# Cross-attention keys in full fp32, made from unsplit weights in pieces between the mixer's small matmuls; the memory scaled once

## The chip, the cores and the metric

The kernel runs on one core of one Trainium2 chip. The metric is device time in microseconds of one execution; one span of the profile is one execution on that core. The program is written engine by engine (TensorE, VectorE, ScalarE, GpSimd, SyncE), with its own order of work on each and semaphores between them.

## The reference, cut to what matters

Two layers of a decoder trunk, for 256 prompt positions and 8 x 4 sample positions (288 columns together), model width 1024:

```
for l in range(DEPTH):                                   # DEPTH = 2
    x = x + 0.5 * swiglu_ffn(rmsnorm(x, ffn1_norm[l]), ...)
    h = rmsnorm(x, mix_norm[l])
    x = x + concat(conv | dilated attention | rwkv7)(h @ w_in[l]) @ w_out[l]
    h  = rmsnorm(x, xattn_norm[l])
    hm = rmsnorm(mem, mem_norm[l])                       # mem (256, 1024): the same in both layers
    mk, mv = split(hm @ w_kv[l], 2, axis=-1)             # keys and values, 1024 columns each; both also outputs
    x = x + cross_attend(h, mk, mv, w_q[l], w_o[l])      # 4 heads of 256, over the 256 memory rows
    x = x + 0.5 * swiglu_ffn(rmsnorm(x, ffn2_norm[l]), ...)
```

`rmsnorm(mem, g)` is `mem * (1 / sqrt(mean(mem**2) + eps)) * g`: only the gain `g` differs from layer to layer. The sample rows take their memory keys and values from caches.

## The kernel before, in words

Everything is held transposed: 128 channels on the partitions, positions along the free axis, so `x` is 8 tiles of 128 x 288 and the memory 8 tiles of 128 x 256. Weights stream in as slabs of 1 MB (128 x 2048 fp32), in one order written out in `ORDER`, through a ring of four slots: SyncE issues slab n when what stood in its slot, slab n-4, has been released, and waits for that before it goes on to the next (L490). A weight slab holds two units of 128 x 1024. ScalarE rounds a unit to a short fp32 form `w_hi` (`CAST w_hi<-slots`) and VectorE makes the rest, `w_lo`; there are three pairs of buffers for them, two more for some units of `out`. The activations are split likewise, and a product is three matmuls: hi by hi, lo by hi, hi by lo (`mm3`, L691 to L693). A split slab is released by VectorE's `w_lo` of its second unit; a slab that is read as it is (the caches `wink`, `winv`, `memk`, `memv`) by TensorE's last matmul on it. `columns` (L744) runs one output tile after another: 8 x `mm3` into a PSUM bank.

The order of one layer on TensorE: ffn1; the mixer's in-projection; the mixer itself, which is small matmuls (rwkv state updates L961 to L1110, convolution and group-norm statistics L1118 to L1150, attention scores L1168, transposes `turn_probs` L1178, `apply_probs` L1189, sample attention on the cached windows L1202 and L1271); then `out_part` and `columns("out")`; then cross attention: key tiles 0 to 3 (`memory_keys`, by `columns`), `sum_squares("xattn")` between the first two, query tiles 0 to 7, the other key tiles, the scores (L1343), the values with the sample scores among them (L1328), softmax, `sample_values` (L1397), the output projection, and ffn2. The small matmuls wait often for ScalarE and VectorE, which evict, exponentiate and normalise between them.

The memory is normalised where the mixer ends. Its squares are summed in the first layer only, by eight full fp32 matmuls between the attention steps (L1224, `memory_squares`). In both layers VectorE then multiplies by root and gain (`normalise("mem", ...)`, L1994 to L2002) and makes `hm_lo` while TensorE does the window values and the first out tiles; the wait for `attn_lo` (the last attention rows' low part), which the attention tiles of `out` need, comes after this in VectorE's order. Full fp32 matmuls appear as two instructions each on TensorE; `x` counts in the trace are of instructions.

Of the kernel before, what the change touches and what calls it, by code (L numbers as in the profile page):

```python
# [38 lines left out]
K_BANKS = (1, 2, 3, 6, 0, 7)  # L39
V_BANKS = (6, 7, 6, 7, 0, 1, 2, 3)  # L40
# [13 lines left out]
MEMK_EARLY = 6  # L54
K_EARLY = 4
# [14 lines left out]
CACHES = ("wink", "winv", "memk", "memv")  # L70
ORDER = [(_name, _i) for _name, _n in STAGES for _i in range(_n)]
# [4 lines left out]
for _i in range(K_EARLY // 2):  # L76
    ORDER.remove(("kv", _i))
    ORDER.insert(ORDER.index(("q", 0)), ("kv", _i))

for _i in range(MEMK_EARLY):  # L80
    ORDER.remove(("memk", _i))
    ORDER.insert(ORDER.index(("kv", _i + K_EARLY // 2)) + 1, ("memk", _i))
PARKED = tuple(("memv", _i) for _i in range(4))
PARKED_BEHIND = {("kv", 4): (0, 1, 2), ("kv", 7): (3,)}
# [6 lines left out]
for _n, (_name, _i) in enumerate(ORDER):  # L91
    if _name not in CACHES:
        UNITS.setdefault(_name, NUNIT)
        UNIT_OF_SLAB[_n] = NUNIT
        NUNIT += 2


def kv_unit(i):
    return UNIT_OF_SLAB[SLAB_AT["kv", i // 2]] + i % 2
# [6 lines left out]
EXTRA_AT = 16384  # L106
# [138 lines left out]
def program(nc, x_in, mem_in, stream, small, consts, conv_hist, wkv_in, copies, outs, known=None):  # L245
    (y_out, conv_out, kv_out, shift_out, wkv_p_out, wkv_s_out, memk_out, memv_out) = outs
    known = known or {}
    with ExitStack() as ctx:
# [26 lines left out]
        rs = sb("rs", [P, T])  # L275
        halves = sb("halves", [P, 2 * J])[:]
# [41 lines left out]

        top[0] = KT * T
        qx = take(KT, T)  # L320
        h_flat, sq_flat = h_mem.rearrange("p a k t -> p (a k t)"), sq.rearrange("p k t -> p (k t)")
        parked = (sq_flat[:, 0:SLAB], h_flat[:, 0:SLAB], h_flat[:, SLAB:2 * SLAB])
# [3 lines left out]

        memx = sq.rearrange("p k t -> p (k t)")[:, 0:KT * MEM].rearrange("p (k t) -> p k t", k=KT)
        top[0] += KT * T
        hm_lo = over("hm_lo", top[0], KT, MEM)
        hm = take(KT, MEM)  # L330
        oxs = hm.rearrange("p k t -> p (k t)")[:, 0:256]
        kx = take(KT, MEM)
        parked += (kx.rearrange("p k t -> p (k t)"),)
        xq_lo = over("xq_lo", top[0], KT, T)
        vx = take(2, 4 * MEM)
        pxT = take(4, 2, TP)
        px = take(9, MEM)


        w_more = tuple(over(name, EXTRA_AT + i * UNIT, UNIT)[:] for i, name in enumerate(("w_more_hi", "w_more_lo")))  # L340
        qz = take(KT, DEC_BATCH * 36)
        qz_own = qz.rearrange("p k (b c) -> p k b c", b=DEC_BATCH)[:, :, :, 0:DEC_SEQ]
        xstat = take(4, 9)
# [72 lines left out]
        assert top[0] <= after_solve  # L416
        top[0] = after_solve
# [36 lines left out]
        mem_landed = sem("mem_landed")  # L454
        parked_landed = [sem(f"parked_landed{i}") for i in range(len(PARKED))]
# [60 lines left out]
        def _(pool):  # L516
# [7 lines left out]
            def presum(l, tag, n):  # L524

                for k in range(1, n):
# [3 lines left out]
                    PL.done(nc.gpsimd.tensor_tensor(sq[:, 0, :], sq[:, 0, :], sq[:, k, :], ALU.add), (tag, "added", k))  # L530
# [3 lines left out]
            for l in range(DEPTH):  # L534
# [3 lines left out]
                if l == 0:  # L538
                    pool.wait_ge(con_landed, 48)

# [34 lines left out]
                pool.wait_ge(scalar_done, SL.value(l, ("u", 1)))  # L575
                pool.dma_start(memx, mem_in).then_inc(mem_landed, 16)
# [18 lines left out]
                pool.wait_ge(vector_done, VL.value(l, ("x_out", 0)))  # L595
                pool.wait_ge(stored, store_value(l, "wkv_s"))
                PL.done(nc.gpsimd.memset(qz, 0.0), "qz_clear")
                presum(l, "xattn", PRESUM["xattn"])
                pool.wait_ge(scalar_done, SL.value(l, ("kx", KT - 1)))
# [61 lines left out]
        def _(pe):  # L661
# [6 lines left out]
            for l in range(DEPTH):  # L668
# [37 lines left out]

                def ffn(tag):
                    for t in range(FT):
# [3 lines left out]
                        for b, o in ((gb, 0), (ub, 1)):  # L712
# [9 lines left out]
                            TL.done(i, (tag, "up" if o else "gate", t))  # L722
                            if (t, o) == ((1, 0) if tag == "ffn1" else (0, 0)):
                                sum_squares(tag)
# [238 lines left out]

                pe.wait_ge(vector_done, VL.value(l, "primed"))
# [41 lines left out]
                for j in range(J):  # L1006
                    for hh in range(2):
# [14 lines left out]
                TL.done(i, ("tok", 2, 2))  # L1022
                claim(5, (SL, ("o", 2)))
                pe.wait_ge(wkv_landed, 16 * l + 16)
                for j in range(J):
# [9 lines left out]
                    else:  # L1035
                        turn(2 + j)
                def value_rows(ct):
# [33 lines left out]
                TL.done(i, "s_xinc")  # L1071
                value_rows(1)
# [12 lines left out]
                claim(7, (SL, ("u", 2)))  # L1085
                pe.wait_ge(scalar_done, SL.value(l, ("r", 2)))
                pe.wait_ge(vector_done, VL.value(l, "s_x"))
                for j in range(J):
                    for hh in range(2):
                        s_ = slice(j * P + hh * HD, j * P + (hh + 1) * HD)  # L1090
                        i = mm(bank[7][0:TS, s_], sm[0:TS, hh, 2, j * TS:(j + 1) * TS], rm2[0:TS, s_], start=True, stop=True)
                TL.done(i, ("u", 2))
                value_rows(2)
                pe.wait_ge(scalar_done, SL.value(l, ("u", 2)))
# [6 lines left out]
                TL.done(i, "s_o")  # L1101

# [11 lines left out]
                def conv_variance():  # L1114
                    claim(7, (SL, "ln_std"))
                    pe.wait_ge(scalar_done, SL.value(l, "conv_sq"))
                    for ch in range(2):
                        i = mm(bank[7][J * 32:, 0:T], ones[:, 0:32], yc2[:, ch, :], start=ch == 0, stop=ch == 1)  # L1118
# [10 lines left out]
                def ln_variance():  # L1129

                    pe.wait_ge(scalar_done, SL.value(l, "ln_sq"))
                    for j in range(J):
                        i = mm(bank[7][j * 32:(j + 1) * 32, 0:T], heads[:, HD - 16:HD + 16], tmp_ln[:, j, :], start=True, stop=True)
# [20 lines left out]
                conv_mean(1)  # L1154
                ln_mean()
                next_states(0)
                conv_variance()
                ln_variance()
                def scores(u):
# [1550 lines left out]
```

## Time and profile before

| | us |
|---|---|
| three runs, median (lowest to highest) | 1635.23 (1634.82 to 1640.63) |
| the profiled execution, span | 1636.5 |
| TensorE busy in it | 1582.2 (97%) |
| VectorE, ScalarE, GpSimd busy | 1067.9, 735.3, 231.4 |
| layer 0: mixer's small matmuls, scores to window values | 377.7 to 441 |
| layer 1: the same | 1182.6 to 1245 |

Stretches of the trace are given as from:to in us from the start of the span. A window's row gives its length, the busy time of every engine with its instruction count, the granted clock of TensorE as a share of full speed (1.00 is 2.4 GHz, 0.50 is 1.2 GHz), the busy share of the DMA engines and what they moved in GB/s. A row of a timeline gives start and length in us, the engine, line and operation, what it writes and reads, how many instructions were grouped, and in brackets the idle time before it with what ended that. A row of waits gives the engine and its line, what it waited for, and the total, the number and the longest of these waits in us. PEld is TensorE's weight load, which runs ahead of the matmuls. A row that groups a line's instructions gives its busy time and mean ns, and behind the bar the idle time before them.

### The profile page before, as it was taken

How to read it: one execution, taken by the hardware profiler on the slowest of the kernel's cores; microseconds unless marked ns; L12 is line 12 of the kernel's file. 1: busy time of each engine (PE TensorE's matmuls, PEld its weight loads, DVE VectorE, ACT ScalarE, POOL GpSimd, SP SyncE). 2: the span in 40 equal slices, each digit the busy share in tenths (PEclk: the TensorE clock that was granted, in tenths of full speed). 3: DMA queues.
4: the chain of work that ended last, by engine and by line, in shares of the span. 5: the costliest groups of instructions: out<-in, count | busy, mean ns of one | idle time of the engine just before them, and what ended most of it. 6: DMA issues, size and time to landing. Idle time of an engine off the chain costs nothing.

```text
span 1636.5 us, 31838 instructions
## 1 busy us (share of the span) xinstructions
PE 1582.2 (97%) x13578; PEld 1499.3 (92%) x13578; DVE 1067.9 (65%) x1654; ACT 735.3 (45%) x1233; POOL 231.4 (14%) x214
## 2 busy tenths in 40 slices
PE   8999999899899999999999999998999999999997
PEld 8999998896799789999999999998858987999997
DVE  5777466978764367775477754678786643777744
ACT  5444357523553354443354433573335434544433
POOL 1000000893010010000010000029801000100000
PEclk9999999998999999999999999999969999999999
DMA  6766754402647754445355667442135478544450
GB/s 228 274 237 251 287 182 136 142 3 87 228 175 284 302 215 162 173 155 181 134 191 204 242 251 282 136 148 86 35 125 206 169 304 319 187 158 176 156 175 35
DMA packets 39980, 303.66 MB, mean 186 GB/s; under 512 B 4832, under 2 KB 4992, under 8 KB 7424
## 3 DMA queue, kind: packets, MB, share of 16 engines
q1 hardware_dynamic: 37504, 288.88, 48.6%
q0 software_dynamic: 2048, 11.17, 2.0%
q8 instruction: 108, 1.77, 0.4%
q10 hardware_dynamic: 288, 1.57, 0.3%
q14 instruction: 32, 0.26, 0.0%
HBM read 291.85 MB, written 36.83 MB: 201 GB/s over the span
## 4 chain that ended last, share of the span: by engine, by line
PE 84%; DVE 8%; ACT 5%; DMA 1%; issue 1%; DVEq 0%; ACTq 0%
PE bank L691 23%; PE bank L693 22%; PE bank L692 22%; PE bank L877 3%; DVE w_lo L1982 2%; DMA slots<-stream 1%; ACT w_hi L1443 1%; PE bank L1397 1%; PE bank L1343 1%; PE bank L1328 1%; PE bank L1380 1%; PE bank L841 1%; PE bank L961 1%; PE bank L704 1%; PE bank L1202 1%
## 5 line engine op out<-in xcount | busy, mean ns | idle before, releaser
L1982 DVE TENSOR_TENSOR w_lo<-slots,w_hi 128x1024 fp32r<-128x1024 f32 x386 | 482.1, 1251 | 339.0 <-ACT w_hi L1443 338.7
L1443 ACT CAST w_hi<-slots 128x1024 fp32r<-128x1024 f32 x390 | 405.9, 1044 | 338.6 <-PE bank L693 298.5
L691 PE MATMUL bank<-h_hi,w_hi 128*128 128x288 f32 x1808 | 540.7, 299 | 13.9 <-DVE h_lo L1941 4.8
L692 PE MATMUL bank<-h_lo,w_hi 128*128 128x288 f32 x1808 | 535.2, 296 | 0.0
L693 PE MATMUL bank<-h_hi,w_lo 128*128 128x288 f32 x1808 | 533.4, 295 | 0.0
L691 PEld LDWEIGHTS bank<-h_hi,w_hi 128*128 128x128 f32 x1808 | 340.6, 188 | 20.4 <-DVE w_lo L1982 5.8
L693 PEld LDWEIGHTS bank<-h_hi,w_lo 128*128 128x128 f32 x1808 | 342.2, 189 | 0.0
L692 PEld LDWEIGHTS bank<-h_lo,w_hi 128*128 128x128 f32 x1808 | 341.3, 189 | 0.3
L693 PE MATMUL bank<-hid_hi,w_lo 128*128 128x288 f32 x704 | 207.7, 295 | 0.0
L692 PE MATMUL bank<-hid_lo,w_hi 128*128 128x288 f32 x704 | 207.3, 294 | 0.0
L691 PE MATMUL bank<-hid_hi,w_hi 128*128 128x288 f32 x704 | 207.1, 294 | 0.0
L1443 ACT COPY arena<-bank 128x256 f32<-128x256 f32 (+7 forms) x224 | 77.5, 378 | 216.7 <-PE bank L693 89.7
L530 POOL TENSOR_TENSOR arena<-arena 128x288 f32<-128x288 f32 x45 | 41.5, 922 | 875.9 <-ACT arena L1493 873.6
L693 PEld LDWEIGHTS bank<-hid_hi,w_lo 128*128 128x128 f32 x704 | 132.1, 188 | 0.0
L691 PEld LDWEIGHTS bank<-hid_hi,w_hi 128*128 128x128 f32 x704 | 132.0, 188 | 0.0
L692 PEld LDWEIGHTS bank<-hid_lo,w_hi 128*128 128x128 f32 x704 | 132.0, 188 | 0.0
L1512 ACT ACTIVATE arena<-arena 128x288 f32<-128x288 f32 x88 | 39.2, 445 | 188.0 <-DVE arena L2021 188.0
L557 POOL TENSOR_SCALAR arena<-arena,par_all 128x256 f32<-128x256 f32 x88 | 101.2, 1161 | 3.9
L2021 DVE TENSOR_TENSOR arena<-bank,rs 128x288 f32<-128x288 f32 x88 | 40.3, 458 | 38.9 <-PE bank L693 38.2
L877 PE MATMUL bank<-arena 64*64 64x64 f32 x1488 | 55.6, 228 | 8.6 <-DVE arena L2251 7.3
L877 PEld LDWEIGHTS bank<-arena 64*64 64x64 f32 x1488 | 52.8, 142 | 11.2 <-DVE arena L2251 7.7
L573 POOL TENSOR_TENSOR arena<-arena 128x512 f32<-128x512 f32 x44 | 61.4, 1395 | 0.3
(350 smaller groups left out, 2274.0 us busy)
## 6 DMA issues: line engine op xcount, KB each, us to landing
slots<-stream SPq DMA_DIRECT2D x235, 1024.0 KB, 5.0
out_win3k<-win3k SPq DMA_DIRECT2D x2, 4080.0 KB
out_win3v<-win3v SPq DMA_DIRECT2D x2, 4080.0 KB
arena<-stream SPq DMA_DIRECT2D x4, 1024.0 KB, 8.1
h_mem<-stream SPq DMA_DIRECT2D x4, 1024.0 KB, 10.0
out_win2k<-win2k SPq DMA_DIRECT2D x2, 2032.0 KB
out_win2v<-win2v SPq DMA_DIRECT2D x2, 2032.0 KB
con<-consts SPq DMA_DIRECT2D x1, 2308.0 KB, 10.7
```

The costliest lines, as they stand in the source:

```text
L530: PL.done(nc.gpsimd.tensor_tensor(sq[:, 0, :], sq[:, 0, :], sq[:, k, :], ALU.add), (tag, "added", k))
L557: p_ = nc.gpsimd.tensor_scalar(out, up[:, ch, tap:tap + TP], w, None, ALU.mult)
L573: PL.done(nc.gpsimd.tensor_tensor(ycv[:, :, 0:TP], ycv[:, :, 0:TP], prod[:, tap % 2, :, 0:TP], ALU.add), ("summed", tap))
L691: mm(out, lhs[0], rhs[0], start=start, stop=False)
L692: mm(out, lhs[0], rhs[1], start=False, stop=False)
L693: return mm(out, lhs[1], rhs[0], start=False, stop=stop)
L704: i = mm(bank[7][:, 0:n], ones, squares[:, k, 0:n], start=k == 0, stop=k == KT - 1)
L877: i = mm(bank[b][o_, s_], lhs[r_, s_], rhs[r_, s_], start=True, stop=True)
L1443: return SL.done(nc.scalar.copy(out, in_), name)
L1512: SL.done(fn(th[:, t % 2, :], gs[:, t % 2, :], ACT.Tanh, scale=0.5), (tag, "tanh", t))
L1982: D(tt(out, src, hi.bitcast(F32), ALU.subtract), name)
L2021: D(tt(gs[:, t % 2, :], bank[gb][:, 0:T], rs[:], ALU.mult), (tag, "gated", t))
```

## The change

**Keys.** The first four `kv` slabs hold the keys' weights; they are now read whole, as the caches are. A key tile is eight matmuls in full fp32, with the 128 x 128 weights as they stand in the slot and the normalised memory `hm` (256 columns) moving. They are issued in pieces by `keys_on(n)` among the mixer's small matmuls, tile 7 first and tile 0 last: 24 before the first scores, 24 up to the last attention step, 8 in front of the wait for `attn_lo`, 8 after the out columns. All tiles but the last share bank 7; ScalarE's `keys_out(t)` copies a tile out, and the next one's first matmul waits for that. `columns("k", ...)`, its 24 matmuls per tile and the splits of its eight units go.

```
@@ TensorE
+                def keys_on(n):
+                    for _ in range(n):
+                        at, k = divmod(piece[0], KT)
+                        t = K_SEQ[at]
+                        b = 7 if at < KT - 1 else 1
+                        if k == 0:
+                            claim(b, (SL, ("kx", t)))
+                        if at == 0:
+                            pe.wait_ge(scalar_done, SL.value(l, ("mem", "h", k)))
+                        w = arrived(SLAB_AT["kv", t // 2]).rearrange("p (o k c) -> p o k c", o=2, k=KT)
+                        i = mm(bank[b][:, 0:MEM], w[:, t % 2, k, :], hm[:, k, :], start=k == 0, stop=k == KT - 1)
+                        piece[0] += 1
+                    if k == KT - 1:
+                        TL.done(i, ("k", "cols", t))
+                        if t % 2 == 0:
+                            TL.done(i, ("slab", SLAB_AT["kv", t // 2]))
...
+                keys_on(2)
                 claim(2, (SL, ("tok", 2, 0)))
...
                 TL.done(i, "s_o")
+                keys_on(2)
@@ ScalarE
+                def keys_out(t):
+                    act.wait_ge(tensor_done, TL.value(l, ("k", "cols", t)))
+                    copy(kx[:, t, :], bank[7 if t != K_SEQ[-1] else 1][:, 0:MEM], ("kx", t))
...
                 value_rows(2)
+                keys_out(6)
                 select(range(2, DEC_BATCH))
```

In TensorE's order this is the place in layer 0 around the sample rows' state (`s_o` is the group with 64x8x4), where a key tile ends and the next begins; before:

```order
L961 MATMUL bank<-arena,con 128x288
L1091 MATMUL bank<-arena 32x64 x6
L1041 MATMUL bank<-con,arena 32x128 x3
L1099 MATMUL bank<-arena 64x8x4 x6
L1049 MATMUL bank<-arena,con 128x288 x2
L1127 MATMUL bank<-arena,con 128x288 x3
```

The key pieces are L1018 in the changed kernel, with two of them behind `s_o`:

```order
L1002 MATMUL bank<-arena,con 128x288
L1018 MATMUL bank<-arena,slots 128x256 x3
L1157 MATMUL bank<-arena 32x64 x6
L1105 MATMUL bank<-con,arena 32x128 x3
L1018 MATMUL bank<-arena,slots 128x256 x2
L1166 MATMUL bank<-arena 64x8x4 x6
L1018 MATMUL bank<-arena,slots 128x256 x2
L1113 MATMUL bank<-arena,con 128x288 x2
L1018 MATMUL bank<-arena,slots 128x256 x2
L1195 MATMUL bank<-arena,con 128x288 x3
```

Eleven pieces have gone before; 3 and 2 complete the second tile (tile 6) ahead of `L1166`; the 17th and 18th behind it begin tile 5 in the same bank, and two more stand between two groups of statistics.

Further on in the same engine's order come the window scores (`slots,arena`), the first transposes and `apply_probs`; before:

```order
L1110 MATMUL bank<-arena 64x512 x2
L1202 MATMUL bank<-slots,arena 32x128 x28
L1178 MATMUL bank<-con,arena 128x128 x3
L1168 MATMUL bank<-arena 128x128 x3
L1189 MATMUL bank<-arena 64x128 x3
L1202 MATMUL bank<-slots,arena 32x128 x14
```

and in the changed kernel:

```order
L1178 MATMUL bank<-arena 64x512 x2
L1273 MATMUL bank<-slots,arena 32x128 x28
L1018 MATMUL bank<-arena,slots 128x256 x7
L1249 MATMUL bank<-con,arena 128x128 x3
L1239 MATMUL bank<-arena 128x128 x3
L1018 MATMUL bank<-arena,slots 128x256
L1260 MATMUL bank<-arena 64x128 x3
L1273 MATMUL bank<-slots,arena 32x128 x14
```

Seven pieces now stand in front of the transposes that wait for the first softmax, and one between the scores and the first `apply_probs`.

**Memory.** The sum of squares moves into ffn1 of layer 0: GpSimd loads the memory, ScalarE squares it, GpSimd adds, one matmul sums over the partitions behind gate tile 17, ScalarE takes the root, VectorE the reciprocal and the product, and GpSimd stores the scaled memory in DRAM once. In each layer ScalarE's queue loads it and ScalarE multiplies by the gain, among the rwkv evictions. The split of `hm`, which the values still use, moves to the out columns.

```
-                normalise("mem", memx, hm, mem_rs, MEM, (hm_hi, hm_lo), between_rows)
+                for u in range(2):
+                    split(UNITS["out"] + NW - 1 + u)
+                dve.wait_ge(scalar_done, SL.value(l, "attn_hi"))
+                low(h_lo[:, 2:2 + G, TP:T], h[:, 2:2 + G, TP:T], h_hi[:, 2:2 + G, TP:T], "attn_lo")
...
+                    dve.wait_ge(scalar_done, SL.value(l, ("mem", "h_hi", t)))
+                    low(hm_lo[:, t, :], hm[:, t, :], hm_hi[:, t, :], ("mem", "h_lo", t))
...
+                act.dma_start(hm, mem_scaled).then_inc(mem_landed, 16)
+                def memory_gained(tiles):
+                    for k in tiles:
+                        act.wait_ge(mem_landed, 16 * l + 16)
+                        g = PAR["mem"] + k
+                        SL.done(fn(hm[:, k, :], hm[:, k, :], ACT.Copy, scale=par_all[:, l, g:g + 1]), ("mem", "h", k))
```

**Order of slabs and values.** The key slabs go between the cache slabs; the values' first two slabs, kv4 and kv5, come before the queries, and the rest after them. Two value pairs are computed before the queries now; after the scores come sample scores 0 and 1, values 2, sample scores 2, values 3, sample scores 3 to 7 in a row.

```
-MEMK_EARLY = 6
-K_EARLY = 4
+MEMK_EARLY = 4
+K_SLABS, V_EARLY = 4, 2
...
+for _i, _next in ((3, ("wink", 0)), (2, ("wink", 2)), (1, ("winv", 0)), (0, ("out", 2))):
     ORDER.remove(("kv", _i))
+    ORDER.insert(ORDER.index(_next), ("kv", _i))
...
-PARKED_BEHIND = {("kv", 4): (0, 1, 2), ("kv", 7): (3,)}
+PARKED_BEHIND = {("kv", 6): (0, 1, 2), ("kv", 7): (3,)}
```

On SyncE the rows of layer 0 from the cache slabs to the parked `memv` slabs (`arena<-stream`, `h_mem<-stream`), with what each issue waits for, were:

```order
L490 DMA slots<-stream 128x2048 [waits vector_done] x20
L490 DMA slots<-stream 128x2048 [waits tensor_done] x8
L490 DMA slots<-stream 128x2048 [waits vector_done] x10
L501 DMA arena<-stream 128x2048 [waits tensor_done]
L501 DMA h_mem<-stream 128x2048 [waits tensor_done] x2
L490 DMA slots<-stream 128x2048 [waits tensor_done]
L490 DMA slots<-stream 128x2048 [waits vector_done]
```

and are now:

```order
L513 DMA slots<-stream 128x2048 [waits vector_done] x20
L513 DMA slots<-stream 128x2048 [waits tensor_done] x11
L513 DMA slots<-stream 128x2048 [waits vector_done]
L513 DMA slots<-stream 128x2048 [waits tensor_done]
L513 DMA slots<-stream 128x2048 [waits vector_done] x7
L524 DMA arena<-stream 128x2048 [waits tensor_done]
L524 DMA h_mem<-stream 128x2048 [waits tensor_done] x2
L513 DMA slots<-stream 128x2048 [waits vector_done]
L513 DMA slots<-stream 128x2048 [waits tensor_done]
L524 DMA arena<-stream 128x2048 [waits stored,tensor_done]
L513 DMA slots<-stream 128x2048 [waits tensor_done]
```

The single `tensor_done` row between two `vector_done` rows is kv5: it goes into the slot of kv0, which TensorE releases with the last key matmul; the four query slabs stand behind it in the queue. Behind kv7 now stand memk3 to memk7; before, memk5 to memk7.

**Banks.** `p_clear` moves from VectorE to GpSimd, the sample rows' `u` and the prompt rows of `apply_probs` use bank 6, the conv and norm variances bank 4, since bank 7 holds the keys.

## Rows read from the trace of the kernel before

**Rows 1.** The page: busy time of the engines, and the chain that ended last.

```profile
PE 1582.2 (97%) x13578; PEld 1499.3 (92%) x13578; DVE 1067.9 (65%) x1654; ACT 735.3 (45%) x1233; POOL 231.4 (14%) x214
...
PE 84%; DVE 8%; ACT 5%; DMA 1%; issue 1%; DVEq 0%; ACTq 0%
```

**Rows 2.** Windows: the mixer's small matmuls up to the first transposes, both layers.

```profile
377.70:414.40 36.70, 33.19 (x343) 21.59 (x342) 31.77 (x81) 16.00 (x33) 4.83 (x7) 0.81 0.40 127
...
1182.60:1222.00 39.40, 36.03 (x342) 23.38 (x342) 31.77 (x81) 16.00 (x33) 4.08 (x6) 0.74 0.36 119
```

**Rows 3.** Windows: the stretches of the mixer in which the clock stood at 0.50.

```profile
385.50:399.10 13.60, 13.60 (x72) 8.32 (x72) 11.20 (x35) 6.00 (x16) 2.38 (x5) 0.50 0.46 162
...
416.20:419.60 3.40, 3.40 (x31) 2.72 (x30) 3.33 (x7) 0.92 (x2) 0.24 (x1) 0.50 0.68 277
1187.60:1208.10 20.50, 20.50 (x125) 12.87 (x127) 14.51 (x42) 7.70 (x19) 3.44 (x5) 0.50 0.30 108
1221.80:1228.60 6.80, 6.57 (x41) 5.38 (x43) 6.32 (x14) 2.79 (x6) 0.56 (x1) 0.50 0.59 239
```

**Rows 4.** Timeline of TensorE, layer 0: first of the split key matmuls, and the 14th.

```profile
468.93 0.28 PE L691 MATMUL bank<-hm_hi,w_hi 128*128 128x256 f32 x1
...
470.48 0.28 PE L692 MATMUL bank<-hm_lo,w_hi 128*128 128x256 f32 x1
```

**Rows 5.** Window of line 1343 alone: sixteen full fp32 matmuls of 128x128 on 256.

```profile
521.70:528.80 7.10, 7.10 (x32) 5.98 (x32) 1.00 0.98 363
```

**Rows 6.** Timeline of TensorE: full fp32 matmuls on 288 columns, three together and alone.

```profile
318.09 1.62 PE L822 MATMUL bank<-arena,con 128*128 128x288 f32 x6
...
380.87 0.75 PE L961 MATMUL bank<-arena,con 128*128 128x288 f32 x2
381.56 1.10 PE L1030 MATMUL bank<-arena 64*64 64x8 f32 x32
```

**Rows 7.** Waits of TensorE's matmuls, 377 to 470 (layer 0).

```profile
PE bank L1178 <- DVE arena L2405: 3.4, 1, 3.4
PE bank L691 <- DVE h_lo L1982: 1.7, 1, 1.7
```

**Rows 8.** Waits of TensorE's weight loads, 377 to 470 (layer 0).

```profile
PEld bank L1091 <- ACT arena L1443: 0.8, 1, 0.8
PEld bank L1069 <- ACT arena L1443: 0.8, 1, 0.8
```

**Rows 9.** Waits of TensorE's matmuls, 1182 to 1275 (layer 1).

```profile
PE bank L1189 <- ACT arena L1443: 1.1, 2, 0.7
PE bank L691 <- DVE h_lo L1982: 0.9, 1, 0.9
```

**Rows 10.** Timeline of TensorE, layer 1: the first transposes.

```profile
1222.03 0.88 PE L1178 MATMUL bank<-con,arena 128*128 128x128 f32 x3 [3.40 <-DVE arena L2405]
```

**Rows 11.** Timeline of ScalarE, layer 0: evictions around the sample state, and a root's table.

```profile
394.09 0.47 ACT L1443 COPY arena<-bank 32x384 f32<-32x384 f32 x1 [1.83 <-PE bank L1091]
394.59 1.12 ACT L1715 ACTIVATE arena<-arena,con 64x384 f32<-64x384 f32 x2
395.64 0.71 ACT L1443 COPY arena<-bank 128x32 f32<-128x32 f32 x4
...
434.92 1.28 ACT L1497 ACT_TABLE_LOAD   x1
```

**Rows 12.** The page: the splits of weight units.

```profile
L1982 DVE TENSOR_TENSOR w_lo<-slots,w_hi 128x1024 fp32r<-128x1024 f32 x386 | 482.1, 1251 | 339.0 <-ACT w_hi L1443 338.7
L1443 ACT CAST w_hi<-slots 128x1024 fp32r<-128x1024 f32 x390 | 405.9, 1044 | 338.6 <-PE bank L693 298.5
```

**Rows 13.** Lines of VectorE: the reciprocal of a root on 288 columns.

```profile
L2013 DVE RECIPROCAL rs<-rs 128x288 f32<-128x288 f32 x4 | 7.8, 1953 | 4.4 <-ACT rs L1499 4.4
```

**Rows 14.** The page: DMA issues of slabs, median us from issue to landing.

```profile
slots<-stream SPq DMA_DIRECT2D x235, 1024.0 KB, 5.0
```

**Rows 15.** Timeline of TensorE: one sample's scores on the memory keys.

```profile
534.53 1.07 PE L1328 MATMUL bank<-slots,arena 128*32 128x256 f32 x16
```

More of the change, by code:

```diff
@@ L91 @@
 for _n, (_name, _i) in enumerate(ORDER):
-    if _name not in CACHES:
+    if not read_whole(_name, _i):
         UNITS.setdefault(_name, NUNIT)
@@ L705, in sum_squares, with memory_sum @@
                     TL.done(i, (tag, "ss"))
+                def memory_sum():
+                    if l:
+                        TL.leave_out(1)
+                        return
+                    claim(7, (SL, ("mem", "rms")))
+                    pe.wait_ge(pool_done, PL.value(0, ("mem", "added", KT - 1)))
+                    TL.done(mm(bank[7][:, 0:MEM], ones, mem_sq[:, 0, :], start=True, stop=True), ("mem", "ss"))
                 def ffn(tag):
@@ L1306, in _, with values @@
                         lambda t: (VL, ("x_out", t)))
[L1309 to L1316 removed]
+                def values(n):
+                    for mt in range(2):
+                        claim(V_BANKS[n * 2 + mt], (SL, ("vx", n * 2 + mt)))
+                    for half in range(2):
+                        u = value_unit(2 * n + half)
+                        hi, lo_ = split(u, KT // 2)
+                        if n == 0 and half == 0:
+                            pe.wait_ge(vector_done, VL.value(l, ("mem", "h_lo", KT - 1)))
+                        for mt in range(2):
+                            for k4 in range(KT // 2):
+                                k, s_ = half * (KT // 2) + k4, slice(mt * P, (mt + 1) * P)
+                                i = mm3(bank[V_BANKS[n * 2 + mt]][:, 0:256], (hm_hi[:, k, s_], hm_lo[:, k, s_]),
+                                        (hi[:, k4, :], lo_[:, k4, :]), k == 0, k == KT - 1)
+                            if mt:
+                                TL.done(i, ("unit", u))
+                            if half:
+                                TL.done(i, ("vx", n * 2 + mt))
+                keys_on(KT)
+                sum_squares("xattn", squares=sqx)
+                for n in range(V_EARLY):
+                    values(n)
                 columns("q", UNITS["q"], range(KT), (xq_hi, xq_lo), lambda k: (VL, ("xattn", "x_lo", k)), range(7),
@@ L2043, in ffn @@
                             split(next_unit(u))
+                            if tag == "ffn1" and half == 0:
+                                memory_scaled(u - middle - 1)
                             if tag == "ffn1" and half == 1 and u == middle + 4:
@@ L2486, in _ @@
                 D(nc.vector.reciprocal(rs[:], rs[:]))
-                for t in range(K_EARLY):
-                    split(next_unit(kv_unit(t)))
+                for i in range(2 * V_EARLY):
+                    split(next_unit(value_unit(i)))
                 for t in range(KT):
@@ L2497, in _ @@
                     split(next_unit(UNITS["q"] + t))
-                for t in range(K_EARLY, KT):
-                    split(next_unit(kv_unit(t)))
                 def two_units(hd):
```

303 lines of the change are left out of this document (162 added, 141 removed).

## The prediction

> **What bounds the kernel now.** I read the page first: TensorE is busy for 1582 of 1636.5 us and holds 84% of the chain that ended last, so time is won by taking work or stops off TensorE; what VectorE and ScalarE are relieved of counts only where TensorE waits for them [rows 1]. The windows come next, since a busy TensorE need not be a fast one: in the mixer's small matmuls, where the key pieces are to go, the granted clock averages 0.81 in layer 0 and 0.74 in layer 1 [rows 2]. It stands at 0.50, the lower level of 1.2 GHz, for 13.6 and 3.4 us in layer 0 and for 20.5 and 6.8 us in layer 1, together 44.3 us; these are the stretches in which the clock can give something back [rows 3]. The two layers do the same work there, and layer 1's window is 2.7 us longer with 20.5 - 13.6 = 6.9 us more at the lower level: a microsecond at it costs 2.7 / 6.9 = 0.39 us, not 0.5, because part of that work waits for other engines anyway. 44.3 us cost 17.3 us. Last come the waits. In layer 0 the first transposes wait 3.4 us for the first softmax and the attention tiles of `out` 1.7 us for the last low part [rows 7]; two weight loads wait 0.8 us each for evictions [rows 8]. In layer 1 there are 3.4 [rows 10], 1.1 and 0.9 us [rows 9].
>
> **The key matmuls.** What goes: 8 tiles x 24 = 192 matmuls on 256 columns. Thirteen of them take 470.48 - 468.93 = 1.55 us from start to start, 0.119 each [rows 4]: 22.9 us per layer. What comes: 64 full fp32 matmuls of the same shape; sixteen such take 7.10 us, 0.444 each [rows 5]: 28.4 us. Full precision is therefore dearer by 5.5 us, not cheaper. They come in 21 groups, and a group that stands alone pays for its seams: one turn takes 381.56 - 380.87 = 0.69 us to the next start, one of three together 1.62 / 3 = 0.54 [rows 6]. Those 0.15 us are the upper end, 0 the lower (a piece whose neighbours have the same 128-row shape may pay nothing); I take 0.1, 2.1 us. Sum per layer: -22.9 + 28.4 + 2.1 = +7.6 us, with bounds +5.5 and +8.7.
>
> A lone warm matmul has, by the Trainium skill (TensorE: Matmul & The Clock Gate, "Single matmul latency"), a fixed part of 398 cycles at full clock, an estimated 0.166 us; if each group paid it, the 21 groups would cost 3.5 us instead of 2.1 and the forecast would rise by 2.8 us over both layers. The 0.15 us of the row is close to it, and speaks for the upper end rather than against the rule.
>
> **The memory's squares.** Eight fp32 matmuls of that shape leave layer 0's attention: 8 x 0.444 = -3.6 us [rows 5]. In ffn1 they become one matmul, +0.44 us; there ScalarE gets eight squares and a root, with a table load of 1.28 us before and another behind it [rows 11], VectorE a reciprocal near 1.95 us [rows 13] and eight products. VectorE is the slower splitter, 1.25 us per unit against 1.04 [rows 12], and ffn1 has TensorE work for some 3.2 us per unit (24 matmuls, each one pass of the four in 0.54, 0.135 us [rows 6]), so three buffers cover this; I take +0.3 us for a late unit, bounds 0 and 1.1. ffn1: +0.7.
>
> **Waits that go.** Seven pieces, 3.1 us, now stand in front of the transposes and fill the 3.4 us; eight, 3.6 us, stand in front of `attn_lo`, and VectorE no longer normalises the memory before it: 1.7 us in layer 0, 0.9 in layer 1. The two short waits on weight loads cost the matmuls about 1.0 us together, and have pieces before them. Layer 0: -3.4 - 1.7 - 1.0 = -6.1. Layer 1: -3.4 - 0.9 - 1.1 - 1.0 = -6.4.
>
> **Waits that come.** (a) Piece 17 stands right behind the sample state `s_o` and begins tile 5 in bank 7, which ScalarE has to empty first. In ScalarE's order that copy stands behind the copies of `s_o` itself, 0.71 us, and the next `value_rows`, 0.47 [rows 11]; with the copy, 0.47 more, TensorE stands still for about 1.7 us, and the conv and norm statistics, on which the softmax and `rwkv_out` of VectorE follow, stand behind it. It is 0 if ScalarE is ahead, and 2.8 if it still has the 1.12 us of the select before `s_o` to do. (b) kv5 goes into the slot of kv0, free after the last key matmul. It lands 5.0 us later [rows 14] and needs 1.04 + 1.25 us of splitting [rows 12], 7.3 us; TensorE has the sum of squares (2 x 0.54) and one value pair (48 x 0.119 = 5.7), 6.8 us. That is 0.5 us; and the root's table load, 1.28, and VectorE's reciprocal, 1.95, stand before the split of kv4's second unit, for another 1.2: 1.7 us, bounds 0 and 5. The queries' slabs wait behind kv5 on SyncE's queue, but four value units of TensorE work cover them. (c) memk7 takes the slot of memk3, which TensorE leaves after the fourth sample's scores; three samples follow at 1.0 us each [rows 15] and the slab needs 5.0 [rows 14]: 2.0 us, bounds 0 and 4. Together 5.4 us per layer.
>
> **Sum at the clock of before.** Layer 0: 7.6 - 3.6 - 6.1 + 5.4 = +3.3. Layer 1: 7.6 - 6.4 + 5.4 = +6.6. ffn1 +0.7. Total +10.6 us.
>
> **The clock.** The lower level comes after stretches of narrow or waiting matmuls: in layer 1 it sets in at 1221.8, as the 3.4 us wait ends whose matmul starts at 1222.03 [rows 3, 10]. The pieces are dense full-width work laid into exactly these places, 48 x 0.444 = 21.3 us of it per layer. I expect them to hold the clock for the most part, and take one stretch of 3.4 us per layer as left; the work in it would lose the full half, 1.7 us each. Gain: 17.3 - 3.4 = 13.9 us. Bounds: 17.3, and less than nothing (rival S).
>
> Net: 10.6 - 13.9 = -3.3 us. Against the profiled execution's 1636.5 that is 1633.2; the median of the runs lies 1.3 lower, so 1631.9. I say 1632 us.
>
> **Rivals.** F, faster: the clock is held all along and none of (a) to (c) comes, because ScalarE runs ahead and slabs land early. 10.6 - 10.8 - 17.3 = -17.5 us, 1618 us. For it: each of the three is a difference of two numbers of similar size. Against it: piece 17 follows the very matmuls whose copies stand ahead of its own release.
>
> S, slower: the clock falls as before in the rwkv part of the mixer, 385 to 400 and 1187 to 1208. There the pieces come one to three at a time, between matmuls of 32 or 64 rows, and the stretches at 0.50 show TensorE busy all through (13.6 of 13.6 and 20.5 of 20.5 us) [rows 3]; so it was not only idle time that preceded them. Then nothing is won back, +10.6 us, 1646; and each piece inside costs another 0.444: with some 29 pieces of both layers there, +12.9, 1659. I put it at 1650. It decides from 10.6 / 0.39 = 27 us won back: with more than 17 of the 44.3 us left, the kernel is slower than before.
>
> By the Trainium skill (TensorE: Matmul & The Clock Gate, "Loop structure matters more than you think") it is waits between matmuls that let the engine go cold and back-to-back work that keeps it warm. The stretch at 1221.8 agrees; the ones at 385.5 and 1187.6, with TensorE busy throughout, are not explained by waits in them. By that rule alone F's clock would hold.
>
> D, the pieces do not lie beside anything: kv3, kv2 and kv1 are now between the cache slabs, so each can be late by a landing of 5.0 us, with the whole mixer behind it in order. Two late slabs per layer are +20 us, 1652. Against it: between the last use of wink1, whose slot kv1 takes, and kv1's first use stand 8 pieces, 3.6 us, and four groups of the mixer's own matmuls.
>
> **Chances.** The forecast, clock mostly held and waits about as computed: 0.45, with its own range 1624 to 1641. F 0.27, S 0.24, D 0.04. What a measurement of this kernel tells from no change is about 0.5%, 8.2 us: faster is below 1627, slower above 1643.4. Of the forecast's 0.45, 0.10 lies below 1627 and 0.35 between; F is all faster; of S, 0.04 ends within; D is slower. Faster 0.37, same 0.39, slower 0.24. Range: F's lower part and S's upper part are cut, 1614 to 1653.
>
> **What would show it.** The key matmuls as 64 per layer at 0.44 us at full clock; windows of the mixer with a granted clock above 0.95; the wait of the first transposes under 0.5 us; a wait near 1.7 us of the second piece group behind `s_o` for ScalarE; the second value unit waiting for VectorE or a slab; a DMA wait near 2 us at the eighth sample's scores. The forecast is wrong if 0.50 stretches of more than 17 us in all remain, or if the new waits are absent or twice as long.

## The result, and the profile after

The changed kernel takes 1655.8 us (median of 4 runs, 1650.3 to 1656.9) against 1635.7 before: ratio 1.0115, 95% interval 1.0098 to 1.0132. In a second series beside other kernels it took 1652.1 against 1637.1, ratio 1.0089 [1.0070, 1.0109]; differences below are taken within that series where a kernel was in it. The block and the versions after it ran in two further series, with the kernel before at 1636.2 and 1636.8, so differences between versions of two series carry up to 1 us of that. It is slower, about as much as rival S gave, but not for rival S's reason. The profiled execution is the fastest of the first four, 1648.5 us of span.

The page first: busy times of the engines, the chain that ended last by engine, and the first lines of it.

```profile
PE 1579.3 (96%) x13436; PEld 1491.3 (90%) x13436; DVE 1045.5 (63%) x1628; ACT 728.5 (44%) x1235; POOL 241.6 (15%) x223
...
PE 81%; DVE 8%; ACT 5%; DMA 5%; issue 1%; DVEq 0%; ACTq 0%
PE bank L722 21%; PE bank L724 20%; PE bank L723 20%; DMA slots<-stream 4%; PE bank L1018 4%; PE bank L918 3%; DVE w_lo L2070 2%; ACT w_hi L1507 2%; PE bank L1444 1%; PE bank L1461 1%; PE bank L1418 1%; PE bank L1273 1%; PE bank L1334 1%; ACT arena L1507 1%; PE bank L882 1%
```

TensorE is busy for 3 us less than in [rows 1] and the span is 12 us longer, so it stands still more. DMA has gone from 1% to 5% of the chain: 4% of it, some 65 us, is now followed back to weight slabs. What the averages hide is where. Windows of the changed kernel, with the columns of [rows 2]: the mixer up to the first transposes in layer 0 and 1, the stretch from the scores to the transposed probabilities of cross attention in both layers, and three short ones of low clock.

```profile
382.70:425.40 42.70, 41.63 (x404) 29.43 (x404) 32.83 (x82) 17.11 (x36) 3.63 (x6) 1.00 0.35 109
...
530.50:567.40 36.90, 28.61 (x256) 22.80 (x256) 10.40 (x19) 8.45 (x23) 0.00 (x0) 0.92 0.83 324
551.10:554.40 3.30, 2.81 (x13) 2.84 (x14) 3.20 (x7) 1.85 (x8) 0.00 (x0) 0.50 0.85 273
564.70:571.50 6.80, 5.38 (x28) 3.44 (x29) 1.17 (x4) 1.85 (x6) 0.00 (x0) 0.50 1.02 433
1191.60:1234.30 42.70, 41.63 (x405) 29.45 (x405) 32.90 (x83) 17.11 (x36) 4.09 (x6) 1.00 0.35 112
1338.80:1375.10 36.30, 28.52 (x256) 22.82 (x256) 10.39 (x19) 8.46 (x23) 0.00 (x0) 0.93 0.82 318
...
213.10:216.50 3.40, 3.40 (x16) 3.40 (x16) 0.83 (x2) 3.08 (x7) 2.39 (x3) 0.50 0.77 267
```

In the mixer the granted clock is 1.00 in both layers, where it was 0.81 and 0.74 [rows 2]: 31 pieces, 13.8 us of work, made these windows only 6.0 and 3.3 us longer. The loss lies behind it, at 0.92 and 0.93, with 8 us of idle TensorE, and in ffn1. The window from the scores to the transposed probabilities had almost no idle TensorE before:

```profile
521.70:558.60 36.90, 36.47 (x325) 32.05 (x321) 15.26 (x23) 13.92 (x31) 0.32 (x1) 1.00 0.81 301
1328.00:1364.80 36.80, 36.37 (x324) 31.98 (x320) 15.17 (x23) 13.84 (x31) 0.29 (x1) 1.00 0.80 303
```

Taking the two traces stage by stage (TensorE's first instruction of each as the mark), with the forecast's terms beside it:

| stage | layer 0, us | layer 1, us | forecast |
|---|---|---|---|
| to the mixer: ffn1 and in-projection (in layer 1 from layer 0's output projection on) | +5.0 | -1.0 | +0.7; 0 |
| mixer to the first out tile (48 pieces) | +10.1 | +7.9 | +12.0; +10.5 |
| out columns, last 16 pieces, two value pairs | +7.6 | +7.8 | +7.3; +8.1 |
| queries (four key tiles gone) | -13.8 | -13.8 | -13.4 |
| scores to transposed probabilities (two value pairs fewer, two samples more) | +0.0 | -0.5 | -7.4 |
| to the output projection | +1.1 | +1.7 | 0 |

The -7.4 are the forecast's prices: two value pairs of 5.7 us fewer, two samples of 1.0 more, 2.0 for memk7. The first, the fifth and the last row hold the error. The waits that stand there, TensorE's matmuls in 120 to 250, 460 to 531 and 530 to 570, columns as in [rows 7]:

```profile
PE bank L722 <- DVE w_lo L2070: 3.1, 1, 3.1
...
PE bank L722 <- DVE w_lo L2070: 2.1, 2, 1.5
...
PE bank L722 <- ACT arena L1948: 5.1, 1, 5.1
PE bank L1405 <- DMA slots<-stream: 3.1, 1, 3.1
```

**In ffn1** the wait names VectorE, but VectorE had been idle itself; ScalarE's timeline shows that the slab was late, and GpSimd's what was put on the DMA engines before that.

```profile
190.33 0.58 POOL L568 DMA_DIRECT2D mem_scaled<-arena  x1 [79.02 <-DVE arena L2134]
```

```profile
210.20 1.04 ACT L1507 CAST w_hi<-slots 128x1024 fp32r<-128x1024 f32 x1 [9.17 <-DMA slots<-stream]
```

The 1 MB store of the scaled memory starts at 190.3, between weight slabs and a window cache's copy that was issued at 178. The slab that SyncE issues at 183.2 lands after 26.9 us, where it took 22.3 before. The unit waited 9.2 us for its slab, TensorE 3.1 us for the unit, and the clock stood at 0.50 right behind it, 213.1 to 216.5.

**Behind the scores**, timelines of TensorE, ScalarE and VectorE, and SyncE's issue of kv7:

```profile
537.60 1.93 PE L1405 MATMUL bank<-slots,arena 128*32 128x256 f32 x32
...
545.40 1.07 PE L1405 MATMUL bank<-slots,arena 128*32 128x256 f32 x16
551.59 0.55 PE L722 MATMUL bank<-w_hi,hm_hi 128*128 128x256 f32 x1 [5.12 <-ACT arena L1948]
...
565.58 1.94 PE L1405 MATMUL bank<-slots,arena 128*32 128x256 f32 x16 [3.14 <-DMA slots<-stream]
```

```profile
538.73 0.33 SPq L513 DMA_DIRECT2D slots<-stream  x1
```

```profile
543.44 1.05 ACT L1507 CAST w_hi<-slots 128x1024 fp32r<-128x1024 f32 x1 [15.67 <-DMA slots<-stream]
544.51 1.28 ACT L1948 ACT_TABLE_LOAD   x1
546.58 0.47 ACT L1948 ACTIVATE arena<-bank,arena 128x256 f32<-128x256 f32 x1 [0.79 <-DVE arena L2606]
```

```profile
544.52 1.23 DVE L2070 TENSOR_TENSOR w_lo<-slots,w_hi 128x1024 fp32r<-128x1024 f32 x1 [14.10 <-ACT w_hi L1507]
545.66 0.68 DVE L2604 TENSOR_REDUCE arena<-bank 128x2 f32<-128x512 f32 x1
```

The scores are done at 537.6. VectorE's row maxima come only at 545.7: it and ScalarE stand 14 and 16 us in front of the split of kv7's first unit, which both have in their order ahead of the softmax. kv7 takes memk0's slot, so it is issued at 538.7, when TensorE has done the first sample. Only then maxima, exponentials, and the banks for the last value pair: 5.1 us. The 3.1 us wait for memk7 is the one foreseen as (c); both are followed by a stretch at 0.50.

### The profile page after: what moved, and what is told of

Read it like the earlier page. It is cut to its first block, busy times and chain, and to the rows that moved or that the text cites. A ratio compares the mean times of both kernels' runs of the same rounds, so it can differ in the third digit from the quotient of the medians.

```text
span 1648.5 us, 31568 instructions
## 1 busy us (share of the span) xinstructions
PE 1579.3 (96%) x13436; PEld 1491.3 (90%) x13436; DVE 1045.5 (63%) x1628; ACT 728.5 (44%) x1235; POOL 241.6 (15%) x223
## 4 chain that ended last, share of the span: by engine, by line
PE 81%; DVE 8%; ACT 5%; DMA 5%; issue 1%; DVEq 0%; ACTq 0%
PE bank L722 21%; PE bank L724 20%; PE bank L723 20%; DMA slots<-stream 4%; PE bank L1018 4%; PE bank L918 3%; DVE w_lo L2070 2%; ACT w_hi L1507 2%; PE bank L1444 1%; PE bank L1461 1%; PE bank L1418 1%; PE bank L1273 1%; PE bank L1334 1%; ACT arena L1507 1%; PE bank L882 1%
## 5 line engine op out<-in xcount | busy, mean ns | idle before, releaser
L2070 DVE TENSOR_TENSOR w_lo<-slots,w_hi 128x1024 fp32r<-128x1024 f32 x370 | 462.9, 1255 | 343.9 <-ACT w_hi L1507 342.2
L722 PE MATMUL bank<-h_hi,w_hi 128*128 128x288 f32 x1808 | 540.6, 299 | 11.7 <-DVE w_lo L2070 5.0
L1507 ACT CAST w_hi<-slots 128x1024 fp32r<-128x1024 f32 x374 | 388.5, 1045 | 362.1 <-PE bank L724 269.3
L553 POOL TENSOR_TENSOR arena<-arena 128x288 f32<-128x288 f32 (+1 forms) x52 | 49.4, 949 | 743.9 <-ACT arena L1557 740.5
L1018 PE MATMUL bank<-arena,slots 128*128 128x256 f32 x256 | 65.0, 390 | 2.1 <-ACT arena L1507 2.1
```

What stands on the lines that cost most here:

```text
L553: PL.done(nc.gpsimd.tensor_tensor(squares[:, 0, :], squares[:, 0, :], squares[:, k, :], ALU.add), (tag, "added", k))
L722: mm(out, lhs[0], rhs[0], start=start, stop=False)
L1018: i = mm(bank[b][:, 0:MEM], w[:, t % 2, k, :], hm[:, k, :], start=k == 0, stop=k == KT - 1)
L1507: return SL.done(nc.scalar.copy(out, in_), name)
L2070: D(tt(out, src, hi.bitcast(F32), ALU.subtract), name)
```

## The experiments

**The control**, the changed kernel unedited.

> 

> The changed kernel itself once more, beside the others. Its one profiled execution so far spans 1648.5 us at a mean granted clock of 0.988, the other three 1653.6 to 1655.1 at 0.982 to 0.984. Theory: the 5 to 6 us between them are further stretches of half clock somewhere, so an execution of 1655 us shows some 10 to 14 us more at 0.50 than the first profile, and the same waits. Rival: a wait that comes and goes (a slab landing late) makes the difference, and the half clock is only its echo; then a new wait of several us is seen.

Its profiled execution took 1653.4 us, 3.1 more than the first, with 52.6 us of the span at 0.50 against 39.4. The waits are the same but for one: at the first value pair of layer 0, 490 to 531, TensorE waits longer.

```profile
PE bank L722 <- DVE w_lo L2070: 3.2, 1, 3.2
```

It was 2.1 us in two waits, and the clock now falls behind it for 3.4 us. So the theory holds in the main: the executions differ in how long the clock stays low behind the same waits, and in part in the length of one wait.

**kv7 early.**

```
-    ORDER.insert(ORDER.index(("kv", 6)) if _i < 2 else ORDER.index(("kv", 4 + _i)) + 1, ("memk", _i))
+    ORDER.insert(ORDER.index(("kv", 7)) + 1 + _i, ("memk", _i))
-PARKED_BEHIND = {("kv", 6): (0, 1, 2), ("kv", 7): (3,)}
+PARKED_BEHIND = {("memk", 1): (0, 1, 2), ("memk", 2): (3,)}
```

> 

> One order is changed: slab kv7 goes directly behind kv6, ahead of the first sample key slabs, so that it takes the slot of a query slab and not that of memk0. Theory (late slab): VectorE and ScalarE split kv7's first unit ahead of the softmax of the prompt's scores, kv7 is issued only when TensorE has left memk0 (538.7) and lands at 543.4, so the row maxima start at 545.7 and the fourth value pair waits 5.1 us for the exponentials that free its banks, and the clock falls behind it. With kv7 early, the 5.1 us wait goes under 0.5 us and the half clock behind it goes too: 6 us less per layer, 11 to 13 us in all. Rival (thin cover): two value pairs after the scores are simply too little work to hide maxima and exponentials, whatever slab comes when; then the wait stays above 3 us and the time changes by less than 4 us.

1641.1 us, 11.0 less than the control (1.0029 [1.0019, 1.0040] of before). Waits of TensorE's matmuls behind the scores of layer 0:

```profile
PE bank L1405 <- DMA slots<-stream: 5.0, 3, 3.1
PE bank L1433 <- ACT arena L1507: 1.3, 2, 0.8
```

The wait for the exponentials is gone, as the late-slab theory has it; the stretch is 4.2 us shorter than in the changed kernel's profile, not 6, because the sample key slabs, now behind kv7, are waited for in three places.

**The store later.** In GpSimd's program the store moves behind the mixer's first `presum` steps (GpSimd adding up squares).

```
                     presum(0, "mem", KT, mem_sq)
-                    pool.wait_ge(vector_done, VL.value(0, ("mem", "scaled", KT - 1)))
-                    pool.dma_start(mem_scaled, memx).then_inc(mem_stored, 16)
...
                 presum(l, "mix", EARLY)
+                if l == 0:
+                    pool.wait_ge(vector_done, VL.value(0, ("mem", "scaled", KT - 1)))
+                    pool.dma_start(mem_scaled, memx).then_inc(mem_stored, 16)
```

> 

> Only GpSimd's order in layer 0 is changed: the store of the scaled memory (1 MB) comes behind the mixer's first two presums instead of in the middle of ffn1's down phase. Theory (contention): the store at 190.3 runs into the copy of a window cache and the slabs, a weight slab takes 27.0 us instead of 22.3 to land, TensorE waits 3.1 us and loses the clock for 3.4 us; with the store later this wait goes, -4 to -5 us. Rival (split queue): VectorE's reciprocal and products, ScalarE's root and table loads make the unit late; then the wait stays and the time is the same within 1 us.

1647.6 us, 4.5 less than the control. The 3.1 us wait is 1.0 now, with no stretch at 0.50 behind it:

```profile
PE bank L723 <- DVE w_lo L2071: 1.0, 1, 1.0
```

So most of it was the store: the slab issued at 183.3 lands after 24.8 us instead of 26.9, and reciprocal, products and table loads are where they were. What the last 1.0 us waits for stays open.

**Both, and the fourth sample earlier.**

```
-                for n in range(V_EARLY, 4):
-                    values(n)
-                    sample_scores(n)
+                values(2)
+                sample_scores(2)
+                sample_scores(3)
+                values(3)
```

> 

> Both edits together, and the fourth sample's scores ahead of the last value pair, so that memk7's slot comes free 6 us earlier. Theory: -11 to -13, -4 to -5, and the wait of 3.1 us for memk7 with its half clock, 4 us per layer, -8: in all 22 to 26 us less than the changed kernel, about 1630. Rival: the slabs are bound together by the bandwidth of the stretch, and one that goes earlier makes another late; then the sum is under 15 us.

1638.3 us (1633.1 to 1644.3), 13.8 less than the control and, within the spread, no more than the 15.5 of the two parts, where 22 to 26 were expected: the rival's figure. The fourth sample now waits 3.5 us for memk3, whose slot VectorE frees late.

**The spreading undone.** All `keys_on` calls go from the mixer; one block stands behind the out columns, each tile in a bank of its own, the key slabs in front of kv4.

```
-                keys_on(KT)
+                for _ in range(KT):
+                    keys_on(KT)
                 sum_squares("xattn", squares=sqx)
```

> 

> The spreading is undone: no key piece stands in the mixer, all 64 full fp32 key matmuls of a layer follow the out columns in one block, and the four key slabs stand there in the stream. The rest is the changed kernel's. Theory (the pieces hold the clock and fill waits): the mixer from its sample state to the first out tile goes back to what it was before less the squares, 59 us in layer 0 and 65 in layer 1 (now 73.2 and 73.2 with 48 pieces, 21.3 us, in it), with a granted clock near 0.8 and the 3.4 us wait for the first softmax; so of the 21.3 us a layer, 7.5 and 13.3 us were free, and the block makes the kernel 20 to 25 us slower than the changed one, some 1672 to 1677. Rival (the pieces only add): the mixer shortens by the pieces' whole 21 us, and the time is within 8 us of the changed kernel's 1652.

1664.1 us, 12.0 slower than the control (1.0169 of before, against 1.0089). Windows: the mixer of layer 0 up to the transposes, and in it the stretch of low clock.

```profile
379.50:417.30 37.80, 34.41 (x343) 22.30 (x342) 31.82 (x81) 16.02 (x33) 4.08 (x6) 0.77 0.31 98
386.40:403.50 17.10, 17.10 (x90) 10.38 (x90) 13.17 (x39) 7.56 (x19) 3.18 (x5) 0.50 0.34 128
```

The low clock and the 3.4 us waits are back. Without its 48 pieces, 21.3 us, the mixer to the first out tile is only 9.6 and 10.8 us shorter, 63.6 and 62.3: the spreading hides 11.7 and 10.5 us, about as much over both layers as the theory said (20.8). The total was put too high. By the stage marks of this profile and the control's, 9.5 us apart, the block's execution is also shorter by 6.5 us at the first value pair, 4.1 ahead of the output projection (half clock), 2.6 in ffn1 and 1.2 because 48 pieces in a row take 20.7 us a layer, and longer by 1.6 behind the scores: 22.2 - 6.5 - 4.1 - 2.6 - 1.2 + 1.6 = 9.4. Which of these the block causes, and which differ from one execution to the next, is not shown.

**No pieces in the rwkv part.**

```
-                keys_on(2)
                 claim(2, (SL, ("tok", 2, 0)))
...
                 conv_mean(1)
-                keys_on(2)
+                keys_on(8)
```

> 

> Only the places of the first 24 pieces are changed: none stands between the small rwkv matmuls; a whole tile of eight stands behind the conv mean, one behind the conv variance, one behind the norm variance, all ahead of the first scores. Theory (each piece holds the clock where it stands): the rwkv part, which ran at 0.50 for 13.6 and 20.5 us before, falls to 0.50 again for 10 us or more a layer, and the stretch up to the first scores grows from 31.3 to 34 us or more; the time rises by 5 to 10 us in spite of the wait behind the sample state, 1.1 us a layer, that goes. Rival (the clock follows the waits, not the narrow matmuls): the rwkv part stays at full clock without pieces, and the kernel gains the 1.1 us a layer, 1650.

1661.5 us, 9.4 slower than the control. Windows of the low clock in layer 0 and 1:

```profile
388.80:402.50 13.70, 13.70 (x80) 8.63 (x77) 11.12 (x34) 5.78 (x16) 3.14 (x5) 0.50 0.46 160
1201.20:1221.70 20.50, 20.50 (x127) 13.75 (x126) 12.96 (x38) 7.13 (x18) 3.44 (x5) 0.50 0.30 108
```

These are the stretches of [rows 3] again, 13.7 and 20.5 us, with TensorE busy throughout by the trace. The same work a few microseconds later does not hold the clock here; the stretch up to the first scores takes 35.6 and 38.7 us instead of 31.3.

**memk0 ahead of kv7**, in the version with both edits and the earlier fourth sample; memv3 behind memk4.

```
+ORDER.remove(("kv", 7))
+ORDER.insert(ORDER.index(("memk", 1)), ("kv", 7))
```

> 

> The third version (both edits and the fourth sample's scores earlier, 1638.3) with memk0 ahead of kv7, and the parked memv3 behind memk4. There memk3 stood in kv7's slot, which is free only when VectorE has split kv7's second unit (539.8); the scores of the fourth sample waited 3.5 us for it and the clock fell for 6.8 us behind. Now memk3 follows memk0, free at 533. Theory: that wait goes under 0.5 us, -3.5 us and the half clock's 2 to 3 us in either layer, 1627 to 1633. Rival (bandwidth): sixteen slabs come in this stretch, another one is late instead, and the time stays above 1636.

1635.8 us (0.9997 [0.9985, 1.0008] of before). That is 2.5 less than the version it starts from, but by the ratios to the kernel before, 1.0002 [0.9988, 1.0016] there, it is not clear of noise. Waits behind the scores of layer 0:

```profile
PE bank L1408 <- DMA slots<-stream: 4.0, 3, 2.0
```

One wait of 3.5 has become three that sum to 4.0. The rival, on the whole (the time is 0.2 us under its bound): what is late changes, that something is late does not.

**Two more waits away.**

```
                 TL.done(i, "s_o")
-                keys_on(2)
...
-                keys_on(2)
+                keys_on(4)
                 ln_mean()
...
+                for tiles in (range(NW, KT - 2), range(KT - 2, KT)):
+                    columns("out", UNITS["out"], tiles, ...)
+                    if tiles[0] == NW:
+                        keys_on(KT)
```

> 

> The version before this one, with two waits of the changed kernel taken away: the two pieces behind the sample state s_o go behind the conv mean (the wait of 1.1 us a layer for ScalarE to empty bank 7), and the last key tile goes from behind the out columns to in front of the last two of them, in bank 7, so that kv5's slot is free some 10 us earlier (a wait of 2.1 us a layer at the first value pair). Theory: -2 and -3 to -4 us against that version, 1622 to 1628, faster than the kernel before by 0.5% or more. Rival: the first value pair waits for the root and the reciprocal, not for kv5; then only the 2 us come.

1634.2 us (0.9987 [0.9979, 0.9996]), 1.6 less than the version before it, and the two intervals overlap. Waits among those of 380 to 560:

```profile
PE bank L738 <- ACT arena L1562: 1.0, 1, 1.0
PE bank L1021 <- DMA slots<-stream: 0.9, 1, 0.9
```

The 1.1 us behind the sample state went (30.3 instead of 31.3 us to the scores), but in layer 0 a key piece now waits 0.9 us for its slab. From the sum of squares to the first query the stage marks show 14.3 us in either layer instead of 16.2 and 14.1, since the sum of squares now waits 1.0 for the last squares. Less than the theory's 5 us, and near the rival's 2.

**The value pairs behind the scores again**, with that version.

```
-K_SLABS, V_EARLY = 4, 2
+K_SLABS, V_EARLY = 4, 0
...
+_tail = [("kv", 4), ("kv", 5), ("memk", 0), ("kv", 6), ("memk", 1), ("kv", 7), *(("memk", _i) for _i in range(2, 8))]
...
+                values(0)
                 sample_scores(0)
+                values(1)
                 sample_scores(1)
```

> 

> The last version with all four value pairs behind the scores again, as in the kernel before, and the sample scores among them: values 0, sample 0, values 1, sample 1, values 2, samples 2 and 3, values 3, samples 4 to 7; kv4 to kv7 and the sample key slabs are ordered so that each takes a slot that is free a value pair before it is needed. TensorE's work is the same. In the version before it the stretch from the scores to the first transposes of the probabilities takes 32.5 us, 27.1 of it work (7.1 + 2 x 5.94 + 8 x 0.94 and the first landing), with waits of 4 us a layer for sample key slabs and half clock behind. Theory (thin cover): two value pairs are too little work for the twelve slabs and the softmax of this stretch; with four, the waits go, 5 us a layer and the half clock behind, 10 to 12 us in all, 1622 to 1625. Rival (the stretch is bound by the slabs' bandwidth whichever way its work is ordered): the waits only move, to the queries or the sample values, and the time stays above 1631.

1622.1 us (1621.0 to 1628.8): 0.9917 [0.9902, 0.9932] of the kernel before, and 12.1 us less than the version before it. Windows from the scores to the transposes of the probabilities, both layers, and the waits there in layer 0:

```profile
511.40:551.20 39.80, 38.41 (x352) 32.80 (x352) 15.45 (x23) 13.21 (x31) 0.00 (x0) 1.00 0.84 316
...
1309.10:1348.80 39.70, 38.28 (x352) 32.86 (x352) 15.45 (x23) 13.26 (x31) 0.00 (x0) 1.00 0.84 311
```

```profile
PE bank L1436 <- ACT arena L1510: 1.8, 2, 1.0
PE bank L1405 <- DMA slots<-stream: 1.4, 1, 1.4
```

TensorE stands still for 1.4 us, against 8 in the changed kernel, and the clock is 1.00. The waits did not move to another place, so the rival fell: the stretch is not bound by its slabs whichever way the work is ordered. The DMA engines are about as busy as in the changed kernel (0.84 against 0.83), with more TensorE work beside them. The edit sets more than the value pairs, though: the order of the slabs, the banks, and the order of splits and softmax on ScalarE and VectorE go with them. Orders of slabs alone got 11.0 us (kv7 early) and at most 2.5 (memk0 ahead of kv7). Whether a slab of the short stretch was late for its slot or for the DMA engines, whose share is 1.02 from 564.7 to 571.5 of the changed kernel, is not separated.

**That edit alone**, in the changed kernel.

> 

> The changed kernel with this one edit alone: the value pairs behind the scores, with that order of slabs; the store in ffn1, the two pieces behind the sample state and the last key tile stay where the changed kernel has them. Theory: the waits for kv7 (5.1 us), memk7 (3.1), kv5 and the root (2.1) and the half clock behind them (2 to 3) go in both layers, a little comes for the second query slab, which now takes kv0's slot: 20 to 24 us less than the changed kernel's 1652, some 1628 to 1632. So this one move of the change would be the larger part of what it lost. Rival: under 12 us, as with kv7 alone (1641).

1635.3 us (0.9993 [0.9981, 1.0004] of before), 16.8 us less than the control. Between theory and rival, nearer the theory: the wait for the exponentials and the low clock behind it are gone, and the sample key slabs cost 1.0 and 1.8 us of waits in the two layers instead of 3.1 and 2.1; but the second query slab, which follows kv0, now costs 4.3 and 4.1 us (30.7 and 30.6 us of queries instead of 26.4), more than the little that was expected. TensorE's wait in 489 to 521, and ScalarE's for the slab:

```profile
PE bank L720 <- ACT arena L1508: 2.4, 1, 2.4
493.67 1.04 ACT L1508 CAST w_hi<-slots 128x1024 fp32r<-128x1024 f32 x1 [6.90 <-DMA slots<-stream]
```

So this one move of the change, with the orders that belong to it, cost some 17 us, as much as the whole loss: without it the kernel takes the time of the kernel before.

## Why the prediction was wrong

- **Price of the keys: right.** Seven pieces together take 3.1 us at full clock (422.29 to the next matmul at 425.42), 0.45 each. The mixer with its 48 came out at +10.1 and +7.9 us, 1.9 and 2.6 below the forecast's terms.
- **Clock: the mechanism right, its size a little short.** All of the mixer's 44.3 us at 0.50 went, not 37.5. That the pieces do it where they stand is shown by the versions without them: none in the rwkv part, and the 13.7 and 20.5 us are back. Rival S, that pieces in ones to threes would not hold it, fell.
- **Waits that go: right but for one.** The first transposes wait for nothing, nor do the attention tiles of `out` for `attn_lo`. The 1.1 us of `apply_probs` in layer 1 [rows 9] were counted as gone; it waits 1.0 us there still, and now 1.0 in layer 0 too.
- **(a) 1.7 us, measured 1.1; (b) 1.7, measured 2.1; (c) 2.0, measured 3.1 and 2.1 in the two layers.** All three came, near their size; that the clock falls behind a wait, and the work there takes longer, had no term.
- **The step that failed: "Waits that come" behind the scores was taken to be memk7 alone.** The change moved two of four value pairs out of this stretch, and the forecast counted that as nothing but moved work. They had been the cover for the slabs that land there and for the softmax. kv7, in memk0's slot and ahead of the softmax in two engines' orders, has no term in the prediction. Instead of 7.4 us shorter the stretch came out as long as before: 7.4 and 6.9 us more than forecast, and 1.1 and 1.7 us of low clock up to the output projection, 17 us over both layers. The version with this move alone taken back is 16.8 us faster.
- **The second: ffn1's +0.7 counted engines, not the queue.** The load and the store of 2 x 1 MB were no term; the store cost 4.5 us, by the version that moves it. What the load costs is not shown.
- The sum: forecast -3.3; ffn1 +4.3 more, behind the scores +17.1 more, the mixer 4.5 less, layer 1's ffn1 1.0 less, the rest 0.8 less on balance: +11.8, against 12.0 between the two profiled spans. The medians lie further apart. The other three executions of the first series have a mean granted clock of 0.982 to 0.984, the profiled one 0.988; the control's trace, at 0.984, shows the low clock staying longer behind mostly the same waits.

The rest of the change, fp32 keys in pieces and the memory scaled once, can thus be a gain: with the value pairs back, the store out of the way and two small waits removed, the kernel beats the one before by 0.83%. How much of that is the keys' alone no version shows.

## What to carry to other kernels

Dense matmuls laid between narrow ones can be nearly half free: 21.3 us of them cost 9.6 and 10.8 here, because they fill waits and hold the clock. But work that moves is also cover that goes: for each stretch that loses work, list the slabs that have to arrive in it, whose release each waits for, and which splits stand ahead of its softmax in the other engines' orders. A DMA that is issued once counts against the copies that run in the same microseconds.

## What was not expected of the hardware

The low clock is not only a matter of idle time: it came back for 13.7 and 20.5 us in stretches in which TensorE is 100% busy by the trace, mostly with narrow matmuls, and with one to three full-width fp32 pieces between them it stood at 2.4 GHz (granted clock 1.00 over 42.7 us). By the Trainium skill (TensorE: Matmul & The Clock Gate, "Loop structure matters more than you think") long waits between bursts are what turns the engine cold. The stretches behind the waits of 3 to 5 us agree with it; the 13.7 and 20.5 us show no such wait. And a short wait can cost more than its length: 5.1 and 3.1 us of waits were followed by some 10 us at 0.50 in layer 0, and the way to the output projection took 1.1 us more behind them.
